# A two-block transformer on one core: the last expert's result stays on chip, the others are fetched sooner, and the walk over spare expert blocks moves ahead of the last eight experts

## The reference, cut to what matters

```python
def hier_moe(x, ...):                 # x: 512 tokens in layer 0, 256 in layer 1, 1024 wide
    ...                               # each token takes 2 of 32 experts, with weights top_w
    hdn = silu(xb @ w_gate[e]) * (xb @ w_up[e])
    ys  = hdn @ w_down[e]             # rows of the tokens of expert e
    return segment_sum(ys[dest] * w_sorted[:, None], order // TOP_K, num_segments=t)

h = h + gt2 * y                       # end of a layer
...                                   # next layer: rms_norm(h) @ w_in, second block: rms_norm(h, g_final), ...
```

## Time and profile before

| | |
|---|---|
| median of 3 runs | 2800.45 us (2787.35 to 2803.42) |
| profiled execution | 2802.77 us, span 2800.9 us |
| PE busy | 2498.2 us, 89% of the span |
| DVE, ACT, POOL busy | 738.2, 468.7, 174.4 us |
| HBM to and from | 245 GB/s over the span |
| chain that ended last | PE 69%, DMA 25%, DVE 2% |

### The profile page before, as it was taken

One profiled execution on the slowest core, in us unless ns is written; L12 is line 12 of the kernel. 1 busy time (PEld: TensorE's weight loads), 2 busy tenths in 40 slices (PEclk: granted clock), 3 DMA queues, 4 the chain that ended last, 5 costly groups with the idle time before them and its releaser, 6 DMA issues.

```text
span 2800.9 us, 30130 instructions
## 1 busy us (share of the span) xinstructions
PE 2498.2 (89%) x12058; PEld 1507.6 (54%) x12058; DVE 738.2 (26%) x1539; ACT 468.7 (17%) x1039; POOL 174.4 (6%) x200
## 2 busy tenths in 40 slices
PE   6999999999987777779999999777776999998998
PEld 3444445445544444335577664444443778885873
DVE  1675444214200000054244230000002333212210
ACT  2120323101110000022122111000001212202320
POOL 0000000000111111110000011111100000000000
PEclk8999999999999999989999999999998999999999
DMA  7354110333899999854523599999985323243441
GB/s 316 132 228 180 60 61 31 151 120 149 354 425 426 426 427 425 367 230 171 219 91 130 208 371 423 425 426 426 425 371 195 136 105 120 106 152 148 150 150 60
DMA packets 60279, 666.38 MB, mean 238 GB/s; under 512 B 12820, under 2 KB 12980, under 8 KB 21008
## 3 DMA queue, kind: packets, MB, share of 16 engines
q1 hardware_dynamic: 44896, 630.48, 55.4%
q0 software_dynamic: 14416, 31.30, 3.0%
q10 hardware_dynamic: 864, 3.15, 0.3%
HBM read 664.81 MB, written 21.02 MB: 245 GB/s over the span
## 4 chain that ended last, share of the span: by engine, by line
PE 69%; DMA 25%; DVE 2%; issue 1%; ACT 1%; SPq 0%; POOL 0%; POOLq 0%; DVEq 0%; ACTq 0%
DMA ring<-in_w_moe 16%; PE act_bank L638 7%; PE act_bank L649 7%; PE act_bank L735 5%; PE act_bank L1099 5%; PE vec_bank L751 4%; DMA xT<-in_w_moe 4%; PE vec_bank L907 4%; PE score_bank L735 4%; PE vec_bank L735 3%; PE score_bank L996 3%; PE vec_bank L1006 3%; PE act_bank L1327 3%; PE vec_bank L1327 3%; PE vec_bank L1345 3%; DMA heads<-in_w_moe 3%
## 5 line engine op out<-in xcount | busy, mean ns | idle before, releaser
L638 PE MATMUL act_bank<-ring,xT 128*128 128x512 f32 x448 | 198.6, 601 | 3.4 <-ACT xT L1452 3.4
L649 PE MATMUL act_bank<-xT,ring 128*128 128x512 f32 (+1 forms) x512 | 193.6, 539 | 0.0
L2293 DVE TENSOR_TENSOR heads<-work,vec_bank 128x256 f32<-128x256 f32 x64 | 27.0, 421 | 538.9 <-PE vec_bank L996 538.9
L735 PE MATMUL act_bank<-xT,ring 128*128 128x256 f32 (+1 forms) x576 | 157.8, 427 | 1.9 <-issue 1.5
L649 PEld LDWEIGHTS act_bank<-xT,ring 128*128 128x128 f32 x512 | 97.1, 190 | 95.5 <-issue 92.3
L996 PE MATMUL score_bank<-ring,branches 128*64 128x256 f32 x1024 | 120.6, 389 | 30.8 <-issue 17.5
L996 PE MATMUL vec_bank<-ring,branches 128*64 128x256 f32 x1024 | 117.2, 381 | 28.9 <-DMA ring<-in_w_moe 28.9
L638 PEld LDWEIGHTS act_bank<-ring,xT 128*128 128x128 f32 x448 | 85.3, 193 | 106.9 <-issue 102.1
L1006 PE MATMUL vec_bank<-ring,heads 128*64 128x512 f32 x512 | 116.9, 598 | 28.7 <-DMA ring<-in_w_moe 23.5
L735 PEld LDWEIGHTS act_bank<-xT,ring 128*128 128x128 f32 x576 | 109.2, 190 | 44.1 <-issue 32.0
L2307 DVE COPY work<-vec_bank 128x512 f32<-128x512 f32 x64 | 44.3, 692 | 328.2 <-PE vec_bank L1006 328.2
(11 more groups left out here) (380 smaller groups left out, 3319.7 us busy)
## 6 DMA issues: line engine op xcount, KB each, us to landing
ring<-in_w_moe SPq DMA_DIRECT2D x96, 2048.0 KB
ring<-in_w_in SPq DMA_DIRECT2D x31, 2048.0 KB
ring<-in_w_merge SPq DMA_DIRECT2D x27, 2048.0 KB
ring<-in_w_ada SPq DMA_DIRECT2D x24, 2048.0 KB
branches<-in_w_moe SPq DMA_DIRECT2D x24, 2048.0 KB
heads<-in_w_moe SPq DMA_DIRECT2D x24, 2048.0 KB
xT<-in_w_moe SPq DMA_DIRECT2D x24, 2048.0 KB
values<-in_w_moe SPq DMA_DIRECT2D x24, 2048.0 KB, 37.0
```

The lines of the kernel that those rows point to most:

```text
L638: mm = pe.matmul(b.t[:, :], xT[:, k, tile * P:(tile + 1) * P], w[:, k * COLS:(k + 1) * COLS], start=(k == 0), stop=(k == KD - 1))
L649: mm = pe.matmul(b.t[:, 0:n], w[:, k * COLS + f * P:k * COLS + (f + 1) * P], xT[:, k, 0:n], start=(k == 0), stop=(k == KD - 1))
L735: mm = pe.matmul(g.t[:, 0:n], merge_tile(l, i, MERGE_TILES * d + k), xs[:, k, 0:n], start=(k == 0), stop=(k == KD - 1))
```

## The change

Three things change.

1. The result of expert 31 is no longer scattered to DRAM. DVE scales it by `gt2` on the way out of the bank (`last_rows`); a matrix that holds each token's weight at its place in expert 31 (`last_places`, turned by PE in `turn_places`) is multiplied with it on PE (`last_sum`, two products for each tile, into `V[0]` and `V[1]`), and DVE adds these to `h` in `combine`. The rows of expert 31 in `y_rows` are set to zero once, at the start of the stage, by a scatter of zeros.
2. `results(l)` waits for the scatters of experts 0 to 30 and for the up product of expert 31, and then loads the first tiles. ACT takes one of the multiplications of `combine` (`scaled`), and the squares are taken in halves. SP's `results_first` stands ahead of U in layer 1 and ahead of the first chunk of the second block.
3. The walk over the further blocks comes after expert 23 on all engines.

```diff
+        def last_sum(l, tile):
+            s = tile // 2
+            if s < streams(l) - 1:
+                pe.wait_ge(last_scaled.sem, l + 1)
+            else:
+                pe.wait_ge(*mark["last_read", l])
+            for g in range(2):
+                pe.wait_ge(V[g].free, V[g].fills)
+            for g in range(2):
+                rows = slice(g * CAP, (g + 1) * CAP)
+                pe.matmul(V[g].t[:, :], placedT[rows, tile, :], last_y[s][rows, :], start=True, stop=True)
...
+            def next_tile(tile):
+                norm_tile(l, tile)
+                if l >= 1 and tile + 1 < NT:
+                    last_sum(l - 1, tile + 1)
+            if l >= 1:
+                last_sum(l - 1, 0)
+            next_tile(0)
...
+        def scaled(l, tile):                       # ACT
+            nc.scalar.activation(y, y, ACT.Copy, scale=weight[:, tile, 0:1])
...
+        def last_rows(l, s):                       # DVE
+            ins = TT(last_y[s], o.t[:, :], gt2_halves[:, s, :], ALU.mult)
...
         def combine(l, tile):
-            step(TS(y[:, 0, :], y[:, 0, :], weight[:, tile, 0:1], None, ALU.mult))
+            dve.wait_ge(y_scaled.sem, y_scaled.take("dve"))
             step(STT(out=y[:, 0, :], in0=y[:, 1, :], scalar=weight[:, tile, 1:2], in1=y[:, 0, :], ...))
             step(TT(y[:, 0, :], y[:, 0, :], gt2b[:, tile // 2, :], ALU.mult))
-            TT(h[:, tile, :], h[:, tile, :], y[:, 0, :], ALU.add)
+            step(TT(h[:, tile, :], h[:, tile, :], y[:, 0, :], ALU.add))
+            for g in range(2):
+                dve.wait_ge(V[g].full, V[g].reads + 1)
+                TT(h[:, tile, half], h[:, tile, half], V[g].t[:, :], ALU.add)
...
         def results(l):                            # POOL
             for b in range(2):
-                pool.wait_ge(scattered[b], 16 * (N_EXP // 2) * (l + 1))
+                pool.wait_ge(scattered[b], 16 * (N_EXP // 2 - b) * (l + 1))
+            pool.wait_ge(zeroed, 16 * (l + 1))
+            pool.wait_ge(*mark["last_up", l])
             for tile in range(tiles(l)):
+                if tile == NT - 1:
+                    pool.wait_ge(*mark["moe_end", l])
                 pool.dma_start(y_tile[tile], y2[tile * P:(tile + 1) * P, :])
...
-                    if l >= 1 and c == ("in", l, "V"):     # SP
+                    if l >= 1 and c == ("in", l, "U"):
                         results_first(l)
```

More of the change, by code:

```diff
@@ L1033, in expert, with turn_places @@
             down_product(o, b, ring[s[2]]).then_inc(o.full, o.fill())
+        def turn_places(l):
+            b = A[0]
+            pe.wait_ge(place_done.sem, place_done.take("pe"))
+            pe.wait_ge(b.free, b.fills)
+            for tile in range(tiles(l)):
+                mm = pe.transpose(b.t[:, tile * P:(tile + 1) * P], placed[:, tile, :], ident)
+            mm.then_inc(b.full, b.fill())
         def experts(l):
@@ L1049, in experts @@
             turns.done(n_turn - 1)
[L1050 to L1054, removed]
+            mark["moe_late", l] = at_bank(V[3])
             with further_blocks(pe, l) as j:
@@ L1068, in experts @@
                 pe.wait_ge(s["dve"], 2 * j + 2)
+            turn_places(l)
+            for q in range(MOE_AHEAD):
+                last = n_turn - 1
+                expert(l, q, lambda r: loads(q, r, last),
+                       g0 + (q + 1) // 2 + 1 + MOE_AHEAD // 2 * last if q < MOE_AHEAD - 1 else None)
+            mark["last_up", l], mark["moe_end", l], mark["last_read", l] = at_bank(V[1]), at_bank(V[3]), let_go(V[3])
         def norm2_tile(tile):
@@ L1119, in second_in @@
         def second_in():
+            last_sum(DEPTH - 1, 0)
             norm2_tile(0)
+            last_sum(DEPTH - 1, 1)
             for q in range(2):
@@ L2293, in expert, with last_places @@
             TT(hid[:, b, :], silu_s[:, b, :], V[b].t[:, 0:D_HALF], ALU.mult).then_inc(V[b].free, V[b].read())
+        def last_places(l):
+            nt, r = tiles(l), r_area[l]
+            pos, blk = r["pos"], r["blk"]
+            chosen, at, w, slot = [r["w1"][:, :, a:b] for a, b in ((0, 2), (2, 4), (4, 5), (5, 6))]
+            step(TS(chosen, blk, float(N_EXP - 1), None, ALU.is_equal))
+            step(STT(out=at, in0=pos, scalar=1.0, in1=chosen, op0=ALU.add, op1=ALU.mult))
+            step(TT(chosen, chosen, weight[:, 0:nt, :], ALU.mult))
+            step(nc.vector.tensor_reduce(w, chosen, X, ALU.add))
+            step(nc.vector.tensor_reduce(slot, at, X, ALU.add))
+            step(TS(slot, slot, 1.0, None, ALU.subtract))
+            halves = C("places")[:, 0:CAP].unsqueeze(1).to_broadcast([P, 2, CAP])
+            for tile in range(nt):
+                ins = TS(placed[:, tile, :].rearrange("p (h n) -> p h n", h=2), halves, slot[:, tile, :], w[:, tile, :],
+                         ALU.is_equal, ALU.mult)
+            ins.then_inc(place_done.sem, place_done.up())
+        def last_rows(l, s):
+            o = V[3]
+            dve.wait_ge(o.full, o.reads + 1)
+            dve.wait_ge(gt2_in[l], 32 * streams(l))
+            ins = TT(last_y[s], o.t[:, :], gt2_halves[:, s, :], ALU.mult)
+            if s < streams(l) - 1:
+                ins.then_inc(last_scaled.sem, last_scaled.up())
+            else:
+                ins.then_inc(o.free, o.read())
         def experts(l):
+            last_places(l)
             for b in range(2):
@@ L2328, in experts @@
                 dve.sem_inc(s["passed"], 1)
+            turn(last)
         def combine(l, tile):
@@ L2887, in experts @@
                 sp.sem_inc(s["passed"], 1)
+            for c in range(3 * (N_EXP - MOE_AHEAD), 3 * N_EXP):
+                load(("expert", l, c))
         def results_first(l):
```

112 lines of the change are left out of this document (81 added, 31 removed).

## The result

| | before | after |
|---|---|---|
| median of 22 runs each, same chip in turn | 2800.32 us | 2792.11 us (2787.18 to 2796.23) |
| ratio | | 0.9979, 95% interval 0.9972 to 0.9985 |
| span of the profiled execution | 2800.9 us | 2791.7 us |
| mean granted clock of PE | 0.970 | 0.973 |

The changed kernel is faster, but by some 6 to 8 us (5.9 by the ratio, 8.2 by the medians) and not by the 17.3 us of the forecast. It is inside the predicted range (2773 to 2797) and next to the time of rival A, 2793.

What follows compares the result with a forecast made beforehand. It took DMA to bound layer 0's expert stage from some 80 us after its start, and the change to work on two stage ends: 8.5 + 8.8 = 17.3 us off 2802.8 gave 2785.5, forecast as 2784, range 2773 to 2797.

Steps and rivals of the forecast that it cites:

- rival A: U or a bank comes late: U 4.6 us late, last_sum at full-array price; gain about 9, 2793 us; chance 0.18.
- Part 1: Layer 0's end: the load of the results lands at 1186.0 instead of 1199.9, 13.9 us earlier.
- rival C: Results come no sooner because the scatter of expert 30 or a late chunk sets the load; 2787 us; chance 0.06.
- Part 2: From the landed results to layer 1's first product: 12.45 us, before 11.0; that product starts 12.4 us sooner.
- Part 4: Load of U for layer 1, issued at 1186.0, lands at 1197.4, hidden by 1 us; cost 0, bounds 0 and 4.
- Part 3: Layer 1's start: PE's added last_sum pairs and the gating product's wait for its bank cost 3.9 us.
- Part 5: Layer 1's end: results land sooner and the second block's first product starts earlier; gain 8.8 us.
- Part 6: Walk after expert 23: PE stalls 12 us, covered by loads in flight; cost 0, bounds 0 and, without cover, 20.4.
- rival B: The walk is not covered and DMA engines fall idle: 2806 us fully, chance 0.07; 2795 in part, chance 0.06.
- Part 7: Start of the expert stage: last_places, the zero scatter and the gt2 row loads cost 0 us, bound 1.2.
- Sum: Whole kernel: gains of 8.5 us at layer 0's end and 8.8 at layer 1's, 17.3 us together.

Runs made afterwards that it cites:

- e1: Also the first experiment: the changed kernel, with PE's wait for U at layer 1's start moved directly ahead of its first product; 2784.44 us, ratio to before 0.9957.
- g3: On top of e1, tile 3's last_sum pair put behind tile 0's gating product, which DVE reads ahead of tile 3's additions; 2779.30 us, ratio to before 0.9932.
- h1: g4 with the walk over further blocks put behind the last expert again on all engines; 2788.26 us, ratio to before 0.9954.
- g4: The edits of g2 and g3 together, on top of e1; 2775.97 us, ratio to before 0.9922.
- e4: On top of e1, the walk cut to one round in place of 15 and 7; 2784.62 us, ratio to before 0.9955.
- g2: On top of e1, gt2 factors taken from the chip without their loads, and the scatter of zeros moved behind the walk; 2779.91 us, ratio to before 0.9938.

## Why the prediction was wrong, point by point

**Part 1, the load of the results.** The three things that it waits for were right: POOL issues it when the up product of expert 31 ends. The time was 1186.3 instead of 1180.2, for reasons in front of it: 1.9 us from the start of the stage, 0.4 from before it, 1.7 of the late V chunk and 1.7 of its slow clock (5.36 against 3.67), and 0.4 of rounding and issue. They come from other parts. The late V chunk is what rival C named ("a late chunk sets the load"), with 1.7 us where C had 1.2 for a late scatter.

**Part 2, the way.** 12.45 us and 0.3 for a pair forecast; 13.0 measured in the first experiment. Right, once U's wait is out of the way.

**Part 4, U: the step that failed.** "With an even split of 2.1 MB each U needs 9.9 + 1.5 = 11.4 us: 1197.4. Hidden, by 1 us." The transfer is right (11.96 measured, and begun 5 us later). "Hidden" is wrong: I compared the landing with the first product that reads U, and Part 2 has `last_rows` and the first `last_sum` "ready at about 1188.5" at no cost. PE's wait for U stands ahead of `last_sum` in PE's queue; so landing + 10.2 us (addition, squares, norm, turning) is the start of the first product, and not landing. Cost: 9.1 us, measured by moving that one wait in e1. The prediction did name "without that cover they would cost under 3 us"; it took the price of the work and not of what is queued in front of it. Rival A had U late, with 4.6 us, by a slower transfer; its time came out (2793) by the wrong mechanism.

**Part 3, PE's additions.** The mechanism is right: the gating product waits for its bank, 1.29 us where 1.8 were forecast (2.7 less the pair's own 0.9), and the stretch of U, V and VA grew by 2.2 us in e1 (63.49 - 61.29) where 3.6 were forecast. But these 2.2 hide a gain that is none of the edit's: the first 24 records of U take 12.36 us before, partly at the lower clock, and 10.57 in e1. From the end of these records to the end of VA it is 49.1 us before, 53.1 in the kernel after and in e1, and 51.6 in g3. So PE's additions cost 4.0 us, a little more than forecast, and the bank was 1.5 of them. A pair takes 1.06 us in the chain and not 0.9. The Trainium skill, TensorEngine Tiling (Array Packing), Tiling Modes, has row tiles work in parallel and a drain at a change of mode. The 1.06 us agree with the first, and by them the drain is 0.2 us at most, an estimate (1.06 less 0.9). But the sentence "the trace has no product of half the rows" was false: the attention of the kernel before has pairs of exactly this kind, four records with their price, which I passed over because they read other tensors (timeline of PE of the kernel before; the clock was granted at 1.00 around the first and at 0.66 on average behind the second):

```profile
1385.88 1.13 PE L794 MATMUL score_bank<-heads 64*128 64x512 f32 x4 [0.52 <-issue]
1388.57 2.74 PE L794 MATMUL score_bank<-heads 64*128 64x512 f32 x4 [1.56 <-ACT work L1537]
```

Four full-array records take 1.8 us by the earlier trace rows. So halves of the rows run side by side, and 1.13 us was there to be read in place of the bounds 0.9 and 1.8.

**Part 5, layer 1.** Forecast 8.8, measured 8.2. Here nothing stands ahead of `last_sum(DEPTH - 1, 0)` in `second_in`, the first chunk's wait comes behind it, and the part came out. The contrast of the two layers is the same finding once more.

**Part 6, the walk.** Covered, as forecast, with PE idle for 9.2 us (12 forecast) and the loss made up in four experts; rival B has fallen. What goes with it and was not forecast is the late V chunk.

**Part 7, the start.** Forecast 0, bound 1.2, measured 2.0 to 2.5. The step that failed here is "with the bus nearly idle". The loads are issued from 715.75 on and land 8 us later, when the DMA share is at 1.02, and what is lost up to expert 8 doesn't come back: it stands 2.1 us later than before, and expert 28 stands 2.0. The bound was too low as well, for these loads cost about twice the time of their bytes.

**Sum.** -17.3 forecast, -9.2 in the profile. The difference by the stretches of the table: +5.7 up to the end of layer 0's last up product, +8.9 in the way behind it (U's wait), +0.6 in layer 1's. Against these stand -2.3 in layer 1 up to its experts (U, V and VA grew by 3.0 in the kernel after, 4.0 less 1.0 that the first 24 records took less at a better clock; behind them 1.7 us less went to the lower clock), and two gains that no part of the change explains: -1.6 in layer 1's stage, where the late and slow chunk of before is missing, and -3.2 in the second block, whose code is the same and where the clock alone gave them (last section). So of the 9.2 us between the two profiles 3.2 are luck with the clock, and the 2.7 us of better clock in layer 1 can't be put down to the change from one profile each.

## What to carry to other kernels

When an operation is put at the head of a stage, read what the engine's queue already waits for there: a wait for a slot, written for the product that reads it, holds up whatever is put behind it, and its price is the whole chain behind the new operation and not the rest of the transfer. Where two waits lie side by side, price the pair and each alone before either is judged by itself. And before a duration is called absent from a trace, look for it by shape of the operands, over the whole program and not under the tensors of the change; loads at the head of a stage that DMA bounds are not free because the first slots are: here 0.52 MB in four loads cost 2.0 to 2.5 us.

## What the runs showed of the hardware

Walking past an empty body costs the engines different times: in h1 14 steps from round to round take DVE 7.4 us (1187.9 to 1195.3) and PE's sequencer 10.7 us (1184.4 to 1195.1).

The same work with the same idle times got different clocks. At the start of layer 1's attention PE stands for 0.52 and 1.56 us in all eleven kernels alike. Behind it the clock falls to its lower level for a while in nine of the eleven kernels, before among them, and stays at full speed in g3 and g4. Windows of e1, then of g3:

```profile
1376.00:1382.00 6.00, 4.83 (x22) 3.25 (x20) 0.65 (x2) 2.05 (x3) 0.00 (x0) 1.00 0.27 57
1382.00:1392.00 10.00, 9.09 (x23) 5.99 (x24) 3.46 (x8) 3.17 (x9) 0.00 (x0) 0.66 0.42 177
```

```profile
1374.00:1380.00 6.00, 4.89 (x22) 3.30 (x20) 0.59 (x1) 2.05 (x3) 0.00 (x0) 1.00 0.24 49
1380.00:1390.00 10.00, 9.03 (x38) 6.27 (x39) 5.23 (x13) 3.88 (x10) 0.00 (x0) 1.00 0.43 183
```

PE is busy 4.83 and 4.89 of 6 us ahead of it, and then the clock is 0.66 in one and 1.00 in the other. Summed over 100 us around this place, (1 - clock) x time is 3.4 us in before and five others, 1.7 in the kernel after, e4 and g2, and 0 in g3 and g4. Such steps can't be put down to a change from one profiled execution each; so the terms above are read from distances inside a stage and not from totals. What decides them is open.

The second block, whose code no kernel here changes, shows what they add up to. It takes 671.6 us before, 668.4 in the kernel after, 665.5 in e1 and 671.9 in h1. Summed over windows of 10 us, (1 - clock) x time in it is 18.4, 15.2, 12.0 and 16.8 us. What is left is 653.2, 653.2, 653.5 and 655.1.
